# A two-block transformer on one core: the order of VectorE's steps at the end of the first block's layers, and four smaller edits

## What is computed

```python
for l in range(2):                                   # first block
    proj = x @ w_in[l]                               # 1024 -> 6816 columns
    merged = gates * (neighbourhood, differential, latent attention) @ w_branch[l]
    x = layer_norm(ALPHA * x + merged @ w_out[l], ln1)
    gu = x @ w_ffn_in[l]                             # 1024 -> 2 * 2816
    ffn = (silu(gu[:, :2816]) * gu[:, 2816:]) @ w_ffn_out[l]
    x = layer_norm(ALPHA * x + ffn, ln2)
for i in range(2):                                   # second block
    h = rms_norm(x) @ w_in_2[i]                      # q, k, v, u, vv
    x = x + merged(attention, spatial gating) @ w_o_2[i]
    h = conv3(rms_norm(x) @ w_up_2[i])
    x = x + (silu(gate) * up) @ w_down_2[i]
```

## Time and profile before

| what | value |
|---|---|
| median of 3 runs | 1495.82 us |
| the profiled execution, its own time | 1495.67 us |
| its span, first to last instruction | 1494.2 us |
| TensorE (PE) busy | 1465.1 us, 98% |
| VectorE (DVE) busy | 1003.1 us, 67% |
| ScalarE (ACT) busy | 784.9 us, 53% |
| mean granted TensorE clock | 1.000 |
| PE's share of the chain that ended last | 82% |
| DVE's share of it | 10% |

### The profile page before, as it was taken

One profiled execution on the slowest core, in us unless ns is written; L12 is line 12 of the kernel. 1 busy time (PEld: TensorE's weight loads), 2 busy tenths in 40 slices (PEclk: granted clock), 3 DMA queues, 4 the chain that ended last, 5 costly groups with the idle time before them and its releaser, 6 DMA issues.

```text
span 1494.2 us, 18393 instructions
## 1 busy us (share of the span) xinstructions
PE 1465.1 (98%) x7191; PEld 1203.8 (81%) x7191; DVE 1003.1 (67%) x1349; ACT 784.9 (53%) x1124; POOL 64.1 (4%) x100
## 2 busy tenths in 40 slices
PE   7999999999999999999999999999999999999998
PEld 5788887888887787887878887788888888888887
DVE  5656885864556655885865555877766668777765
ACT  3565644443443555745344333686655557756553
POOL 2000000000001000000010000210000012000000
PEclk9999999999999999999999999999999999999999
DMA  8544643575564535552765664436555644455551
GB/s 317 188 155 131 237 170 124 171 241 182 184 209 156 203 116 158 183 169 85 234 214 174 201 190 169 142 115 195 184 182 169 197 151 158 155 166 187 170 188 66
DMA packets 167317, 260.99 MB, mean 175 GB/s; under 512 B 8768, under 2 KB 106720, under 8 KB 166720
## 3 DMA queue, kind: packets, MB, share of 16 engines
q1 hardware_dynamic: 166048, 252.03, 51.6%
q0 software_dynamic: 896, 6.74, 1.2%
q10 hardware_dynamic: 288, 1.05, 0.2%
HBM read 258.74 MB, written 1.05 MB: 174 GB/s over the span
## 4 chain that ended last, share of the span: by engine, by line
PE 82%; DVE 10%; ACT 4%; issue 2%; POOL 1%; DMA 1%; SPq 0%; DVEq 0%; ACTq 0%
PE ps L384 15%; PE ps L388 15%; PE ps L386 15%; PE ps L457 10%; PE ps L459 9%; PE ps L458 9%; DVE wlo L1500 3%; ACT whi L1069 2%; PE ps L1001 1%; PE ps L511 1%; PE ps L534 1%; PE ps L414 1%; DVE x L1519 1%; DVE x L1517 1%; PE ps L524 1%
## 5 line engine op out<-in xcount | busy, mean ns | idle before, releaser
L1500 DVE TENSOR_TENSOR wlo<-raw,whi 128x2048 fp32r<-128x2048 f32 (+1 forms) x238 | 528.2, 2229 | 275.0 <-ACT whi L1069 274.4
L1069 ACT ACTIVATE whi<-raw 128x2048 fp32r<-128x2048 f32 (+1 forms) x238 | 441.7, 1865 | 204.7 <-PE ps L388 124.9
L384 PE MATMUL ps<-whi,xTh 128*128 128x512 f32 x704 | 277.4, 394 | 0.0
L388 PE MATMUL ps<-whi,xTl 128*128 128x512 f32 x704 | 274.4, 390 | 0.0
L386 PE MATMUL ps<-wlo,xTh 128*128 128x512 f32 x704 | 274.1, 389 | 0.0
L457 PE MATMUL ps<-whi,xTh 128*128 128x512 f32 (+3 forms) x640 | 251.1, 392 | 7.4 <-DVE xTl L1538 3.4
L459 PE MATMUL ps<-whi,xTl 128*128 128x512 f32 (+3 forms) x640 | 242.1, 378 | 0.0
L458 PE MATMUL ps<-wlo,xTh 128*128 128x512 f32 (+3 forms) x640 | 241.4, 377 | 0.0
L388 PEld LDWEIGHTS ps<-whi,xTl 128*128 128x128 f32 x704 | 132.1, 188 | 27.9
L384 PEld LDWEIGHTS ps<-whi,xTh 128*128 128x128 f32 x704 | 132.2, 188 | 27.6 <-issue 0.8
L386 PEld LDWEIGHTS ps<-wlo,xTh 128*128 128x128 f32 x704 | 132.3, 188 | 26.4
(11 more groups left out here) (185 smaller groups left out, 1635.2 us busy)
## 6 DMA issues: line engine op xcount, KB each, us to landing
raw<-in_w_in SPq DMA_DIRECT2D x124, 512.0 KB, 4.6
raw<-in_w_ffn_in SPq DMA_DIRECT2D x88, 512.0 KB, 4.8
raw<-in_w_up SPq DMA_DIRECT2D x88, 512.0 KB, 4.9
raw<-in_w_ffn_out SPq DMA_DIRECT2D x44, 512.0 KB, 4.4
raw<-in_w_down SPq DMA_DIRECT2D x44, 512.0 KB, 4.6
raw<-in_w_branch SPq DMA_DIRECT2D x24, 512.0 KB, 4.6
raw<-in_w_out SPq DMA_DIRECT2D x16, 512.0 KB, 4.5
raw<-in_w_o SPq DMA_DIRECT2D x16, 512.0 KB, 4.5
```

The source lines that it names most:

```text
L384: PE.matmul(o, ah, hi[:, j, b], start=first and kt == 0, stop=False)
L388: mm = PE.matmul(o, al, hi[:, j, b], start=False, stop=last and j == c - 1 and i == len(kts) - 1)
L1069: AC.activation(m.whi[:, i % SPLIT, 0:w], m.raw[:, slot, 0:w], ACT.Copy).then_inc(s.w_hi, 1)
L1500: DV.tensor_tensor(m.wlo[:, i % SPLIT, 0:w], m.raw[:, slot, 0:w], m.whi[:, i % SPLIT, 0:w].bitcast(F32), ALU.subtract).then_inc(s.w_lo, 1)
```

## The change

Five edits. (1) VectorE's list at the end of a first-block layer gets another order: `add_down(0)` and `stats(0)` come ahead of the split of the next piece; `apply` is cut into `center` (line 1517 before) and `scale_up` (line 1519 before); the first `center` is issued ahead of `hidden_half(1)`; `add_down(1)` comes behind both remainders of half 0 and behind two splits instead of one. TensorE turns quarter (0, 0) ahead of `down(end)` half 1 instead of in its middle. (2) Where x is scaled block by block, VectorE counts up after each of the four instructions, and TensorE waits for each block at its own kt. In the second block's passage between its layers `turn_x(0, 1)` moves behind the last `down` product. (3) `conv_turn` of chunk 0 is issued at kt 3 instead of kt 2. (4) In the neighbourhood attention ScalarE rounds no piece between two copies in the last group. (5) The first half of x is loaded as two transfers, one on SyncE's queue and one on ScalarE's, and the second half of x behind the second transfer of w_in's second row block.

```diff
-    SP.dma_start(m.x[:, 0, :], t["x"][0, 0:P, :]).then_inc(s.x_in, 16)
+    SP.dma_start(m.x[:, 0, 0:512], t["x"][0, 0:P, 0:512]).then_inc(s.x_in, 16)
...
         load_piece(w1[:, 0:4, 0:512], 4, 512)
+        load_piece(w1[:, 4:8, 0:512], 4, 512)
         if not L:
             SP.dma_start(m.x[:, 1, :], t["x"][0, P:S, :]).then_inc(s.x_in2, 16)
-        load_piece(w1[:, 4:8, 0:512], 4, 512)
...
     def x_ready(th, kt):
-        if kt in (0, 4):
-            PE.wait_ge(s.turn_lo, x_lo[th, kt // 4])
+        count, remainders = x_lo[th, kt // 4]
+        if remainders == 4:
+            PE.wait_ge(s.turn_lo, count - 3 + kt % 4)
+        elif kt in (0, 4):
+            PE.wait_ge(s.turn_lo, count)
...
+        last_use = 1 if L + 1 < DEPTH else 4
...
         def first_x_turn(th, kt):
-            if kt == 1:
-                turn_x(0, 0)
+            if kt == 0:
+                turn_x(0, 0, remainders=last_use)
 
         down(end - 1, (1,), last_half_turn)
         h_ready()
         down(end, (1,), first_x_turn)
-        turn_x(0, 1)
+        turn_x(0, 1, remainders=last_use)
...
         def down_turn(th, kt):
             if kt == 1:
-                for n4 in range(2):
-                    turn_x(0, n4)
+                turn_x(0, 0, remainders=4)
 
         def first_conv_turn(th, kt):
-            if (th, kt) == (0, 2):
+            if (th, kt) == (0, 3):
                 bank_free(2)
                 conv_turn()
...
+        if L + 1 < DEPTH:
+            turn_x(0, 1, remainders=4)
...
+    AC.dma_start(m.x[:, 0, 512:D], t["x"][0, 0:P, 512:D]).then_inc(s.x_in1, 16)
     AC.dma_start(m.vec[:, 0:D], t["ln_g"][0:1, :].broadcast_to([P, D])).then_inc(s.vec, 16)
...
-            catch(1, L, "na", g, 2, ahead=SPLIT - (g == 4))
+            catch(1, L, "na", g, 2, ahead=0 if g == 4 else SPLIT)
...
-            a = DV.scalar_tensor_tensor(out=m.xTl[:, kt, o], in0=ps[:, 4 + 2 * th + n4, kt % 4 * P:(kt % 4 + 1) * P],
-                                        scalar=m.pcol[:, col + kt:col + kt + 1], in1=m.xTh[:, kt, o].bitcast(F32), op0=ALU.mult,
-                                        op1=ALU.subtract)
-        a.then_inc(s.turn_lo, 1)
+            DV.scalar_tensor_tensor(out=m.xTl[:, kt, o], in0=ps[:, 4 + 2 * th + n4, kt % 4 * P:(kt % 4 + 1) * P],
+                                    scalar=m.pcol[:, col + kt:col + kt + 1], in1=m.xTh[:, kt, o].bitcast(F32), op0=ALU.mult,
+                                    op1=ALU.subtract).then_inc(s.turn_lo, 1)
...
         later = k.after[1, L, "dn", NSTEP - 1]
         hidden_half(0)
         h_lo(slice(0, P), 2)
-        split_to(later + 1)
         add_down(0, (1, L, "dn", NSTEP - 1))
-        hidden_half(1)
         for n4 in range(2):
             stats(0, n4)
+        split_to(later + 1)
+        DV.wait_ge(s.vec, 32 * (L + 2))
+        center(0, 0)
+        hidden_half(1)
+        scale_up(0, 0)
         h_lo(slice(P, S), 2)
-        DV.wait_ge(s.vec, 32 * (L + 2))
-        apply(0)
+        center(0, 1)
+        scale_up(0, 1)
         if L + 1 < DEPTH:
             turn_lo_quarter(0, 0)
         else:
             DV.wait_ge(s.par, 80)
             turn_lo_gains(0, 0, 16)
         split_to(later + 2)
-        add_down(1, (1, L, "dn", NSTEP - 1))
         if L + 1 < DEPTH:
             turn_lo_quarter(0, 1)
         else:
             turn_lo_gains(0, 1, 16)
+        split_to(later + 3)
+        add_down(1, (1, L, "dn", NSTEP - 1))
         for n4 in range(2):
             stats(1, n4)
-        split_to(later + 3 + (L + 1 < DEPTH))
+        if L + 1 < DEPTH:
+            split_to(later + 4)
         apply(1)
```

More of the change, by code:

```diff
@@ L52 @@
     "free0", "free1", "free2",
-    "x_in", "x_in2", "par", "vec", "lay", "gate_b", "gate_b2", "ln_in", "stored",
+    "x_in", "x_in1", "x_in2", "par", "vec", "lay", "gate_b", "gate_b2", "ln_in", "stored",
     "init",
@@ L408, in gate_cols, with turn_quarter @@
         return m.gate[:, th, kt * P:(kt + 1) * P]
-    def turn_quarter(src, th, n4):
+    def turn_quarter(src, th, n4, remainders=1):
         bank = ps[:, 4 + 2 * th + n4, :].rearrange("p (k s) -> p k s", k=4)
@@ L415, in turn_quarter, with turn_x @@
         mm.then_inc(s.turned, 1)
-        return n.up("turn_lo")
-    def turn_x(th, n4, ready=None):
+        return n.up("turn_lo", remainders)
+    def turn_x(th, n4, ready=None, remainders=1):
         if ready:
@@ L424, in turn_x @@
             PE.wait_ge(s.normed, n.up("normed"))
-        x_lo[th, n4] = turn_quarter(x_cols, th, n4)
+        x_lo[th, n4] = turn_quarter(x_cols, th, n4, remainders), remainders
     def x_ready(th, kt):
-        if kt in (0, 4):
-            PE.wait_ge(s.turn_lo, x_lo[th, kt // 4])
+        count, remainders = x_lo[th, kt // 4]
[3 more added lines that the diff above has]
+            PE.wait_ge(s.turn_lo, count)
     x_lo = {}
@@ L858, in x_ready_turn @@
             if kt in ((1, 2), (5, 6))[L == 0]:
-                turn_x(1, kt - (1, 5)[L == 0])
+                turn_x(1, kt - (1, 5)[L == 0], remainders=4)
         for i, (name, kts, width, th, before) in enumerate((("q", (4, 4), 512, 0, x_ready), ("k", (8,), 256, 0, x_ready_turn),
@@ L986, in out_turn @@
             if kt in (1, 2):
-                turn_x(0, kt - 1, (2, L, "a", kt - 1))
+                turn_x(0, kt - 1, (2, L, "a", kt - 1), 4)
         for i, (j, th, before) in enumerate(((0, 0, outputs_ready), (1, 0, None), (0, 1, out_turn), (1, 1, None))):
@@ L1021, in up_turn @@
                 n4 = kt // 2 - 1
-                turn_x(1, n4, (2, L, "a", n4))
+                turn_x(1, n4, (2, L, "a", n4), 4)
             x_ready(th, kt)
@@ L1510, in stats, with center, scale_up, apply @@
             DV.bn_aggr(m.mv[:, th, :], m.bn[:, th, :, :].rearrange("p a b -> p (a b)")).then_inc(s.moments, 1)
-    def apply(th, n4s=(0, 1)):
-        if 0 in n4s:
+    def center(th, n4):
+        if n4 == 0:
             DV.wait_ge(s.rstd, n.up("rstd"))
[L1515 to L1521, removed]
+        c = slice(n4 * 512, n4 * 512 + 512)
+        then(DV.scalar_tensor_tensor(out=m.x[:, th, c], in0=m.x[:, th, c], scalar=m.mv[:, th, 0:1], in1=m.vec[:, c],
+                                     op0=ALU.subtract, op1=ALU.mult))
+    def scale_up(th, n4):
+        c = slice(n4 * 512, n4 * 512 + 512)
+        DV.scalar_tensor_tensor(out=m.x[:, th, c], in0=m.x[:, th, c], scalar=m.small[:, th:th + 1],
+                                in1=m.vec[:, D + n4 * 512:D + n4 * 512 + 512], op0=ALU.mult,
+                                op1=ALU.add).then_inc(s.normed, 1)
+    def apply(th):
+        for n4 in range(2):
+            center(th, n4)
+            scale_up(th, n4)
     def turn_lo_quarter(th, n4, scale=1.0):
@@ L1742, in vector_program @@
     DV.wait_ge(s.x_in, 16)
-    for n4 in range(2):
-        stats(0, n4)
+    stats(0, 0)
+    DV.wait_ge(s.x_in1, 16)
+    stats(0, 1)
     for L in range(DEPTH):
```

## The result

The changed kernel takes 1501.17 us (median of 9 runs, 1497.95 to 1502.05), the one before 1495.82 us (9 runs beside it, 1495.46 to 1496.29). The ratio is 1.0032 with a 95% interval of 1.0023 to 1.0041 (the medians alone give 1.0036): slower, by 5.4 us. That is outside the predicted range, and it is the time of rival (b), 1501.3 us, which had a chance of 0.07. The profiled execution took 1501.63 us (span 1500.2, mean granted clock 0.995, where it was 1.000 before).

What follows compares the result with a forecast made beforehand. TensorE, busy for 98% of the span, was taken as the bound. Terms 1.3 + 0.8 - 0.4 + 0 + 0 - 0.6 = +1.1 us on 1495.67 gave 1496.8 (1496.9 by the median); range 1494.3 to 1498.9 us.

Steps and rivals of the forecast that it cites:

- rival (b): Both seams: TensorE's clock falls in the new 3.3 us holes, about 2.2 us each; 1501.3 us, chance 0.07.
- The hole: First seam: TensorE waits 3.3 us more for `hidden_half(1)`, its transposes moving from 467.70 to 470.95.
- the seam terms: Cost of the new order of VectorE's list: +1.3 us in the first seam, +0.8 us in the second.
- the wait that I had forecast there at kt 5: Second seam, k product: TensorE reaches kt 5 at 942.2 and waits to 944.9 to turn half 1.
- my own signs of being wrong: Wrong if: transposes at their old time, granted clock below 1.000, start split still at 17.2, or copy on TensorE's path.
- The other rivals of the seam: Beside rival (a): `hidden_half(1)` not late, seams lose waits, 2.2 us at the first, 2.6 second; 1490.0 us, chance 0.05.
- rival (a): Seams: GpSimd is not held or the waits are shorter; +0.5 and 0 there, 1495.3 us, chance 0.2.
- the list ended as walked: First seam: VectorE's list reaches `apply(1)` at 485.5 instead of 484.01, 1.5 us later.
- The start: Start: ScalarE takes the second piece at 14.1 instead of 15.28, product of 23.17 starts at 22.6; -0.6 us.
- The passage: Between the second block's layers: first product 0.87 us earlier, half given back by later k weights; -0.4 us.
- The copy ahead of two roundings: Last neighbourhood attention group: rounding moves behind the copy; 0 in both layers, up to +1 each without cover.
- the second block's feed-forward with the conv turn: Second block's feed-forward: waits by block and the later conv turn, +0.1 and -0.15 us per layer, in sum 0.

Runs made afterwards that it cites:

- experiment 2: The changed kernel with the old order of VectorE's list at the seams and the turn back at kt 1; 1493.73 us, ratio 0.9987.
- experiment 6: The changed kernel with the split moved behind `center`, `hidden_half(1)`, `scale_up` and `h_lo`; 1496.5 us, ratio 1.0004.
- experiment 5: The changed kernel with `hidden_half(1)` ahead of the split and `h_lo` right behind the split; 1497.64 us, ratio 1.0013.
- experiment 3: The changed kernel with 28 idle identity transposes on TensorE in each seam's wait for `hidden_half(1)`; 1497.59 us, ratio 1.0014.
- experiment 1: The kernel before with only the new order of VectorE's list and the earlier turn of (0, 0); 1501.74 us, ratio 1.0041.
- experiment 8: The kernel of experiment 2 with three edits: attention copy in group 3, no split between second conv chunk's copies, k weights' split earlier; 1503.14 us, ratio 1.0043.

## Why the prediction was wrong

**The step that failed.** In the first seam I wrote "So that product starts at 470.95 + 5.3 = 476.2, 2.3 us later". This 5.3 us is a duration at full clock. The hole itself was right: 3.41 us of idle time, and transposes at 470.19 + 0.82 (the gain at the start) = 471.01, where 470.95 was forecast. But from there to the first product TensorE needed 478.22 - 470.19 = 8.03 us; with the hole filled, 475.46 - 470.22 = 5.24, which is my 5.3. So the seam terms, +1.3 and +0.8, are right for a TensorE at 2.4 GHz (+1.34 and +0.72 with both holes filled), and short by 2.8 and 2.8 us for the one that ran (+4.16 and +3.49). The windows give about the same size: a pace below full for 6.7 x 0.46 = 3.1 us' worth in the first seam; in the second 3.6 x 0.38 = 1.4 and 4.5 x 0.38 = 1.7, of which part costs nothing, since TensorE is busy for only 3.97 of those 4.50 us.

**The chance that was wrong.** Rival (b) named place, price and result: two seams, 2.2 us each, 1501.3. I gave it 0.07 because "no row of a hole of this length shows" it. That is no evidence against it. The kernel had no hole of that length at all; its longest wait beside the start's was 1.5 us. The one row that there was spoke for it: after the only long wait, that of the earlier trace rows, TensorE ran at half pace for 4.5 us. (It is the pace that shows it. The clock column has 1.00 for 8.5 to 13.1 us, so at the start of a trace it has to be checked against the length of the products.) The Trainium skill, "TensorE: Matmul & The Clock Gate", section "HAM oscillation — how this bites in real kernels", says that idle gaps between groups of products can let the clock drop and that the next group then starts cold. By that rule, the traces agree: 0.54 over 6.7 us behind 3.41 us without a product. The price of rival (b) was too low, 4.4 us for 5.6: the first seam's fall cost 2.8 us and not 2.2, and the second seam had two falls, not one, since the wait that I had forecast there at kt 5 (2.7 us; 2.60 measured) is a hole as well. That 1501.3 comes so near to 1501.17 is in part luck: the other stages won 1.6 us where I had 1.0, and the median is 0.5 us below the profiled execution. A granted clock below 1.000 stood among my own signs of being wrong.

**What was right.** The other rivals of the seam fell: GpSimd was held (2.12 us, and 0.19 without the split beside it: rival (a) had it the other way), and the list ended as walked, `apply(1)` at 484.83 with the holes filled, or 485.6 without the start's gain of 0.77, for 485.5 forecast. By the rule of the Trainium skill, "SBUF — State Buffer", "Who interferes with whom" (a VectorE instruction with two SBUF inputs and a GpSimd instruction that reads SBUF exclude each other for a whole instruction, and the first to start wins), the trace agrees: the split started at 465.44 and the root's first instruction at 465.61, for 2.12 us.

**The smaller terms.** The start gave 0.82 us for 0.6: ScalarE took the second piece at 13.93 (14.1 forecast), and the first product with the third piece came at 22.44 (22.6). The passage itself gave 0.60 for 0.4; the other 0.08 of its column are that layer's feed-forward part. In experiment 2 the first product is 0.85 us earlier than the shift up to there (0.87 forecast), and of the half that I took as given back by the later k weights only 0.29 is. VectorE's split of them starts 0.59 us later than before by that shift (1216.47, against 1216.95 - 1.07) and ends at 1218.75; the first product with them starts at 1218.85, 0.52 us behind the one ahead of it, where it was 0.23. The copy ahead of two roundings gave 0.00 in both layers (the shift of experiment 2 is the same ahead of the attention and behind it, -0.61 us in the first layer and -0.57 in the second), and the second block's feed-forward with the conv turn gave 0.1 in each layer for 0.

**What stays open.** How long a hole must be is not settled, and its length alone does not say it. Behind waits of 1.49 and 1.50 us (experiment 6, one in each seam) the clock stayed. Behind 2.24, 2.60, 2.75, 3.20 and 3.4 us it fell, but in experiment 5 a wait of 2.58 us in the second seam, 15 us behind another fall, had 1.00 behind it. It also differs from run to run of one kernel: the changed one had mean clocks from 0.998 to 0.995, with 1498 to 1502 us. A fall cost 1.5 us in the second seam of experiment 3 (2.24 - 0.72), and 2.8 in the first of the changed kernel, where the clock stayed low for longer; why it does so in one run and not in another (in experiment 1 the same window has 0.75) is open too. So is why the time of the changed kernel differs by 4 us from run to run, beyond that it goes with the clock.

## What to carry to other kernels

On an engine that is 98% busy, a new hole can cost twice: its own idle time, and slower products behind it. So price a moved wait by its length as one hole, not only by the net delay at the end of the stage; two waits of 1.5 us were free of the second price here, one of 3.4 was not. When a result is worse than the walk, read the granted clock by windows before the list is walked again, and fill the hole with idle transposes as a test: if the time falls, the clock was the cause. And look at what stands ahead of the short instruction that the bound engine waits for, also by way of another engine: here a split of 2.3 us, and the root that it held, were ahead of two instructions of 0.4. With the split behind them (experiment 6) the hole was 1.49 us instead of 3.41, but the old order (experiment 2) was still 2.8 us faster.

## What the runs showed of the hardware

Products that compute nothing made the kernel faster: 78 transposes (28 in each seam's first hole, 22 in the second seam's other one) on the engine that bounds it took 4.9 us off (1501.17 to 1496.27). Transposes of the identity were enough to hold the clock: it was 1.00 in the window 466.8 to 470.1, which had next to nothing else on TensorE, and behind it. In this kernel, which has few gaps, the clock fell behind idle times down to 2.24 us (experiments 5 and 8), and it may fall inside the hole (0.90 for 466.8 to 470.1) or only behind it (1.00 for 929.4 to 932.8, then 0.62). Once down, it also delays the engines that wait for TensorE: VectorE's two remainders waited 1.76 and 1.30 us for copies of transposes, where they waited 0.18 and 0.32 us with the holes filled. Some kernels with such holes scatter more: 4.1 us between the fastest and slowest run of the changed kernel and 3.4 us in experiment 5, against 0.9 us with both holes filled and 0.5 us for experiment 2, which has none. Not all do: experiment 6 has a fall of the clock and 0.9 us.
